# A 32-expert clamped-SwiGLU layer: the gate's activation reads PSUM before the clamp, and one product moves ahead of a subtraction

## Chip, cores and metric

The kernel is one launch on 1 core of one Trainium2 chip. The metric is device time in microseconds; lower is better. The engines are named as in the profile: PE (TensorE matmuls) and PEld (its weight loads), DVE (VectorE), ACT (ScalarE), POOL (GpSimd) and SP (SyncE).

## The reference

One decoder layer for 520 tokens (512 of a prompt, 8 sampled): a recurrent branch and an attention branch, merged by an output projection, then a mixture of 32 experts of which each token takes 4. The change lies in the experts and in one step before them. What an expert computes:

```python
gu = t_pad[tok] @ w_up[e] + b_up[e]
a = jnp.minimum(gu[:, :D_FF], 7.0)
u = jnp.clip(gu[:, D_FF:], -7.0, 7.0)
y = ((u + 1.0) * a * jax.nn.sigmoid(1.702 * a)) @ w_down[e] + b_down[e]
```

`D_MODEL` and `D_FF` are 1024, so an expert has 2048 columns of `w_up` (gate and up part) and 1024 of `w_down`: 12 MB of float32, six slots of 2 MB each.

## The kernel before, in words

**Before the experts.** After the attention and the recurrent branch PE multiplies by the output projection, tile of rows by tile of rows (`RT` is 5; tile 0 holds the 8 sampled tokens). DVE adds the residual (`residual`, L2171), ACT squares and takes the root (L1535, L1543), PE turns the rows (L1021) and computes the router's logits (L1032), DVE picks the four experts of each token. In tile 0 the up bias, fetched into `oT` by two DMAs of POOL's queue (L2438, semaphore `bup_in`), is split into a rounded high part (ACT, L1576 and L1577) and a remainder (DVE, L2274); PE adds both to a chunk with one matmul (L1142).

**The experts.** Each expert takes the rows of its tokens (at most 128) and multiplies in float32 by splitting every operand in a rounded high part and a low part (three products for each). The weights come as six slots of 2 MB (`c` = 0 to 5, each in two halves `h`), read by 192 DMAs from SP's queue. For each of the 12 halves ACT rounds the half into a work tile (`high_half`, L1555; the tile names are `xn`, `wide` and `qT` by turns) and DVE subtracts it in place (`low_half`, L2253). Chunks 0 to 3 are the up projection: chunk 0 makes the first 512 gate columns in PSUM bank 0, chunk 1 the matching up columns in bank 1, chunks 2 and 3 the second 512 of each in banks 2 and 3 (PE, L1150, 24 matmuls a chunk). Chunks 4 and 5 are the down projection (L1168, 12 matmuls a half).

The hidden values are made in two halves `hf`:

- `gate_part(n, hf)` (DVE, L2296): minimum with 7 of the gate bank into `AA`.
- `gated(n, hf)` (ACT, L1595): `Gelu_apprx_sigmoid` of `AA` into `SG`, that is a·sigmoid(1.702a).
- `hidden_part(n, hf)` (DVE): the up bank is clamped to ±7 into `UU[hf]` (L2300), then (UU + 1)·SG in place (L2303).
- PE turns `UU[hf]` (`turn_hidden`, L1132), ACT rounds it (`turned_hidden`, L1599), DVE subtracts (`low_hidden`, L2307).

Nothing schedules this: every engine runs an order written out by hand, with semaphores between them. PE's order for expert `n` (`block_of`) is: chunks 0, 1, 2; turn 0; chunk 3; half (4,0); turn 1; half (4,1); then it waits until both parts of the second hidden half are there (`hh_ready` and `hl_ready` at 2n+2), turns the next expert's rows (`turn_rows`, L1126, 8 transposes) and does (5,0) and (5,1). The wait is written ahead of `turn_rows`:

```python
down_half(n, 4, 1)
pe.wait_ge(S["hh_ready"], 2 * n + 2)
pe.wait_ge(S["hl_ready"], 2 * n + 2)
if following:
    turn_rows(n + 1, 1 - par)
down_half(n, 5, 0)
```

DVE's `hidden_part(n, 1)` waits until PE is through with chunk 3 (`half_used` at 12n + 20). `following` is true for the experts 0 to 30. A branch for an expert with over 128 tokens follows the experts; with these inputs it is not taken.

Of the kernel before, what the change touches and what calls it, by code (L numbers as in the profile page):

```python
# [9 lines left out]
ALU = mybir.AluOpType  # L10
ACT = mybir.ActivationFunctionType
# [8 lines left out]
D = 1024  # L20
# [37 lines left out]
EPS = 1e-6  # L58
LIMIT = 7.0
ALPHA = 1.702  # L60
SLOT = 4096
NSLOT = 6
ROUTER_IN = 96
# [26 lines left out]
def build(nc, d):  # L90
    ctx = ExitStack()
    with ctx:
# [87 lines left out]
        def w8(name):  # L180
# [123 lines left out]
        XH, XL, HH, HL = [slab_r[:, (2 + b) * D:(3 + b) * D].rearrange("p (k t) -> p k t", k=KD) for b in range(4)]  # L304
        XHf, HHf = [slab_r[:, (2 + b) * D:(3 + b) * D].bitcast(F32) for b in (0, 2)]
        YR = [slab[:, (6 + b) * D:(7 + b) * D] for b in (0, 1)]
        AA = slab[:, 8192:8704]
        SG = slab[:, 8704:9216]
        UU = [slab[:, 9216 + b * 512:9728 + b * 512] for b in (0, 1)]
        pick_r = slab_r[:, 10304:10432]  # L310
        pick = causal[:, 0:NE]
# [25 lines left out]
            gate_done gate_out pa_done pb_done m_ready  # L337
            wo_done router_in xm_ready row_norm t_ready x_picked oh_ready t_turned t_copied lg_done ex_in ex_done gd_ready gd_turned
            gd_copied bd_done y0_ready m4_ready pos_done ent_ready table_in scattered bup_in ovf_ready
            bias_hi bias_ready pick_set  # L340
            xg_in ent_in gate_set rows_free x_turned xh_ready xl_ready half_used up_read sig_ready h_ready h_turned hh_ready hl_ready
            wh_ready wl_ready y_scaled y_added
            outs_done""".split()}
# [218 lines left out]
        def _(pe):  # L562
# [570 lines left out]
                r.then_inc(S["h_turned"], 1)  # L1133

            def up_chunk(n, c, last_biases=False):
                pe.wait_ge(S["up_read"], 4 * n + c + 1)
                if c == 0:
                    pe.wait_ge(S["pick_set"], n + 1)
                    pe.wait_ge(S["xh_ready"], n + 1)
                    pe.wait_ge(S["xl_ready"], n + 1)  # L1140
                q = order[c]
                mm(bank[:, c, :], pick_r, bias_r[:, q * 512:(q + 1) * 512], start=True, stop=False)  # L1142
                for h in range(2):
                    pe.wait_ge(S["wh_ready"], 12 * n + 2 * c + h + 1)
                    pe.wait_ge(S["wl_ready"], 12 * n + 2 * c + h + 1)
                    wh = WH[(2 * c + h) % 6].rearrange("p (k n) -> p k n", k=4)
                    wl = ring_r[:, half_of(c, h)].rearrange("p (k n) -> p k n", k=4)
                    for k in range(4):
                        for x, (a, w) in enumerate(((XH, wh), (XH, wl), (XL, wh))):
                            r = mm(bank[:, c, :], a[:, 4 * h + k, :], w[:, k, :], start=False,  # L1150
                                   stop=h == 1 and k == 3 and x == 2)
                    r.then_inc(S["half_used"], 1)
                    if last_biases and h == 0:
                        down_bias(RT - 2, 1)
                        down_bias(RT - 1, 0)
                        down_bias(RT - 1, 1)
# [52 lines left out]
        def _(act):  # L1209
# [347 lines left out]
            for t in range(RT):  # L1557
                if t >= 1:
                    turned_part(t - 1, 1)
                row_squares(t, 0)  # L1560
                if t >= 1:
                    chosen(t - 1)
                if t == RT - 1:
                    fn(lt[:, 0, 0:1], eps1[:, 0:1], ACT.Sqrt)
                turned_part(t, 0)
                if t == RT - 1:
                    turned_gates(t - 1)
                row_squares(t, 1)
                if t == RT - 1:
                    turned_part(t, 1)  # L1570
                row_root(t)
                if 1 <= t < RT - 1:
                    turned_gates(t - 1)
                if t == 0:
                    act.wait_ge(S["bup_in"], 32)
                    fn(bias_r[0:NE, :], bias_raw[0:NE, :], ACT.Copy).then_inc(S["bias_ready"], 1)  # L1576
                    fn(WH[0][NE:2 * NE, :], bias_raw[NE:2 * NE, :], ACT.Copy).then_inc(S["bias_hi"], 1)  # L1577
                if t == 2:
                    act.wait_ge(S["bias_ready"], 3)
                if t in (2, 3):  # L1580
                    high_half(0, 0, t - 2)
# [9 lines left out]
                fn(XH, bank[:, 6:8, :].rearrange("p b (k t) -> p (b k) t", k=4), ACT.Copy).then_inc(S["xh_ready"], 1)  # L1591

            def gated(n, hf):
                act.wait_ge(S["up_read"], 4 * n + 2 * hf + 5)
                fn(SG, AA, ACT.Gelu_apprx_sigmoid).then_inc(S["sig_ready"], 1)  # L1595

            def turned_hidden(n, hf):
                act.wait_ge(S["h_turned"], 2 * n + hf + 1)
# [37 lines left out]
            high_half(0, 1, 1)  # L1636
            high_half(0, 2, 0)
            act.wait_ge(S["bd_done"], 2 * RT)
            block_of(0, 0, True)
            block_of(1, 1, True)  # L1640
            with act.Fori(1, NE // 2 - 1) as pair:
# [15 lines left out]
        def _(dve):  # L1657
# [3 lines left out]
            def one(ins, sem=None):  # L1661

                mine(ins, sem)
                mine.settle()
# [590 lines left out]

            one(v.tensor_tensor(pick, ident[:, 0:NE], ident[:, NE:2 * NE], ALU.add))
            one(v.memset(first_oh[1], 0.0))
            for t in range(RT):
                residual(t, 0)
                if t >= 2:  # L2260
# [9 lines left out]
                row_scale(t)  # L2270
                normalise(t)
                if t == 0:
                    dve.wait_ge(S["bias_hi"], 1)
                    v.tensor_tensor(bias_r[NE:2 * NE, :], bias_raw[NE:2 * NE, :], WHf[0][NE:2 * NE, :], ALU.subtract)\  # L2274
                        .then_inc(S["bias_ready"], 1)
                if t in (2, 3):
# [1 line left out]
            choose(RT - 1)  # L2278
            positions(RT - 1)
            to_weigh(RT - 1)  # L2280
            dve.sem_inc(S["up_read"], 2)

            def low_rows(n):
                dve.wait_ge(S["xh_ready"], n + 1)
# [6 lines left out]
            def pick_expert(e):  # L2291
                v.tensor_copy(pick_r, pick[:, bass.ds(e, 1)].to_broadcast([P, P])).then_inc(S["pick_set"], 1)

            def gate_part(n, hf):
                dve.wait_ge(S["half_used"], 12 * n + 4 * hf + 14)
                v.tensor_scalar(AA, bank[:, 2 * hf, :], LIMIT, None, ALU.min).then_inc(S["up_read"], 1)  # L2296

            def hidden_part(n, hf):
                dve.wait_ge(S["half_used"], 12 * n + 4 * hf + 16)
                v.tensor_scalar(UU[hf], bank[:, 2 * hf + 1, :], LIMIT, -LIMIT, ALU.min, ALU.max).then_inc(S["up_read"], 1)  # L2300
                dve.wait_ge(S["up_read"], 4 * n + 2 * hf + 6)
                dve.wait_ge(S["sig_ready"], 2 * n + hf + 1)
                v.scalar_tensor_tensor(UU[hf], UU[hf], 1.0, SG, ALU.add, ALU.mult).then_inc(S["h_ready"], 1)  # L2303

            def low_hidden(n, hf):
                dve.wait_ge(S["hh_ready"], 2 * n + hf + 1)
# [10 lines left out]
            def block_of(n, e, following, par=None):  # L2317
                low_half(n, 2, 0)
                low_half(n, 2, 1)
                dve.wait_ge(t_out[0], 48)  # L2320
                dve.wait_ge(t_out[1], 32)
                dve.wait_ge(y0_out[2], 16)
                gate_part(n, 0)
                low_half(n, 3, 0)
                low_half(n, 3, 1)
                hidden_part(n, 0)
                low_half(n, 4, 0)
                low_half(n, 4, 1)
                gate_part(n, 1)
                dve.wait_ge(y0_out[0], 32)  # L2330
                low_hidden(n, 0)
                low_half(n, 5, 0)
                low_half(n, 5, 1)
                hidden_part(n, 1)
                if following:
                    pick_expert(e + 1)
                    low_half(n + 1, 0, 0)
# [14 lines left out]
            dve.wait_ge(S["pos_done"], RT + 1)  # L2352
            one(v.tensor_reduce(ovf[:, 0:1], bank[:, 2, 0:NE], AX, ALU.max))
            one(v.tensor_copy(ovf[:, 1:2].bitcast(I32), ovf[:, 0:1]), S["ovf_ready"])
            dve.sem_inc(S["up_read"], 1)
            first_rows(RT - 2, 0)
            low_half(0, 1, 0)
            first_rows(RT - 2, 1)
            dve.sem_inc(S["up_read"], 1)
            low_half(0, 1, 1)  # L2360
            first_rows(RT - 1, 0)
            first_rows(RT - 1, 1)
            with dve.Fori(0, NE // 2 - 1) as pair:
                block_of(2 * pair, 2 * pair, True, 0)
                block_of(2 * pair + 1, 2 * pair + 1, True, 1)
# [306 lines left out]
```

## Time and profile before

| | us |
|---|---|
| median of 3 runs | 1887.18 |
| lowest, highest | 1885.93, 1888.0 |
| span of the profiled execution (first to last instruction) | 1886.3 |
| PE busy | 1827.4 (97%) |
| DVE busy | 1502.2 (80%) |
| ACT busy | 1130.4 (60%) |

For the profiled execution the page gives the span as its time; the median of the runs is 0.9 us above it. The experts take the last 1175 us of the span, from PE's first bias matmul at 712.3 us on. Busy time is a mean over stages with different limits; in a row of a timeline the columns are start, duration, engine, line, operation, what is written and read, and in brackets the idle time of the engine before it with what ended it. The matmuls of a sequence overlap: one of 512 columns lasts 0.39 us in the rows, and the next starts 0.23 us after it.

### The profile page before, as it was taken

How to read it: one execution, taken by the hardware profiler on the slowest of the kernel's cores; microseconds unless marked ns; L12 is line 12 of the kernel's file. 1: busy time of each engine (PE TensorE's matmuls, PEld its weight loads, DVE VectorE, ACT ScalarE, POOL GpSimd, SP SyncE). 2: the span in 40 equal slices, each digit the busy share in tenths (PEclk: the TensorE clock that was granted, in tenths of full speed). 3: DMA queues.
4: the chain of work that ended last, by engine and by line, in shares of the span. 5: the costliest groups of instructions: out<-in, count | busy, mean ns of one | idle time of the engine just before them, and what ended most of it. 6: DMA issues, size and time to landing. Idle time of an engine off the chain costs nothing.

```text
span 1886.3 us, 27452 instructions
## 1 busy us (share of the span) xinstructions
PE 1827.4 (97%) x9813; PEld 1500.9 (80%) x9813; DVE 1502.2 (80%) x1754; ACT 1130.4 (60%) x1126; POOL 239.8 (13%) x259
## 2 busy tenths in 40 slices
PE   7999999999999999999999999999999999999996
PEld 5899988787767677888888888888888888888885
DVE  6865875654367468999999999999999999999994
ACT  5335555442332346767767767776777776776772
POOL 0040000012331131100100110010010010010000
PEclk9999999999999999999999999999999999999998
DMA  5075221132355258999999999999999999999991
GB/s 226 8 247 164 70 78 46 49 94 82 113 167 197 72 199 347 358 396 382 372 381 389 372 375 385 374 377 385 380 372 380 387 370 380 387 374 381 382 365 43
DMA packets 76748, 514.23 MB, mean 273 GB/s; under 512 B 10745, under 2 KB 31297, under 8 KB 50801
## 3 DMA queue, kind: packets, MB, share of 16 engines
q1 hardware_dynamic: 58944, 454.19, 61.4%
q0 software_dynamic: 17584, 58.51, 11.5%
q8 instruction: 46, 0.75, 0.2%
q10 hardware_dynamic: 144, 0.55, 0.1%
q14 instruction: 30, 0.24, 0.0%
HBM read 490.36 MB, written 28.24 MB: 275 GB/s over the span
## 4 chain that ended last, share of the span: by engine, by line
PE 75%; issue 8%; DVE 7%; ACT 6%; DMA 3%; SPq 0%; ACTq 0%; DVEq 0%; POOL 0%; POOLq 0%
PE bank L1150 27%; PE bank L1168 14%; PE bank L700 6%; PE bank L752 5%; PE bank L627 3%; ACT qT_rounded L1555 3%; PE bank L600 3%; PE bank L999 3%; PE bank L1132 2%; PE bank L1126 1%; PE bank L974 1%; DVE slab L2300 1%; DVE slab L2303 1%; PE bank L1142 1%; PE bank L765 1%
## 5 line engine op out<-in xcount | busy, mean ns | idle before, releaser
L2253 DVE TENSOR_TENSOR ring_rounded<-ring,wide_rounded 128x2048 fp32r<-128x2048 f32 x192 | 431.4, 2288 | 50.8 <-ACT wide_rounded L1555 50.3
L1150 PE MATMUL bank<-ring_rounded,slab_rounded 128*128 128x512 f32 x1024 | 400.2, 391 | 0.0
L1555 ACT ACTIVATE wide_rounded<-ring 128x2048 fp32r<-128x2048 f32 x192 | 359.8, 1908 | 10.3 <-PE bank L1150 8.7
L1150 PE MATMUL bank<-xn_rounded,slab_rounded 128*128 128x512 f32 x1024 | 326.3, 389 | 0.0
L2253 DVE TENSOR_TENSOR ring_rounded<-ring,xn_rounded 128x2048 fp32r<-128x2048 f32 x128 | 293.0, 2289 | 17.1 <-ACT xn_rounded L1555 17.1
L1168 PE MATMUL bank<-wide_rounded,slab_rounded 128*128 128x512 f32 x768 | 259.7, 399 | 0.0
L1150 PE MATMUL bank<-wide_rounded,slab_rounded 128*128 128x512 f32 x768 | 247.3, 389 | 0.0
L1555 ACT ACTIVATE xn_rounded<-ring 128x2048 fp32r<-128x2048 f32 x128 | 244.0, 1906 | 0.0
L1150 PEld LDWEIGHTS bank<-ring_rounded,slab_rounded 128*128 128x128 f32 x1024 | 192.2, 188 | 41.3
L1150 PEld LDWEIGHTS bank<-xn_rounded,slab_rounded 128*128 128x128 f32 x1024 | 192.3, 188 | 40.1 <-issue 0.8
L2480 POOL DMA_INDIRECT out_y<-slab,small x32 | 85.0, 2656 | 999.9 <-ACT slab L1630 999.9
L1168 PE MATMUL bank<-ring_rounded,slab_rounded 128*128 128x512 f32 x512 | 200.6, 392 | 0.0
L1599 ACT ACTIVATE slab_rounded<-bank 128x512 fp32r<-128x512 f32 x64 | 38.3, 599 | 221.5 <-PE bank L1132 221.5
L1150 PEld LDWEIGHTS bank<-wide_rounded,slab_rounded 128*128 128x128 f32 x768 | 144.2, 188 | 31.2
L1168 PEld LDWEIGHTS bank<-wide_rounded,slab_rounded 128*128 128x128 f32 x768 | 145.0, 189 | 29.0
L700 PE MATMUL bank<-ring_rounded 128*128 128x260 f32 x768 | 148.1, 292 | 2.3 <-DVE slab_rounded L1873 2.3
L2253 DVE TENSOR_TENSOR ring_rounded<-ring,qT_rounded 128x2048 fp32r<-128x2048 f32 x64 | 146.5, 2290 | 0.9
L700 PEld LDWEIGHTS bank<-ring_rounded 128*128 128x128 f32 x768 | 117.9, 188 | 16.7 <-issue 11.9
L1555 ACT ACTIVATE qT_rounded<-ring 128x2048 fp32r<-128x2048 f32 x64 | 122.3, 1912 | 1.9 <-PE bank L1082 1.9
L1168 PEld LDWEIGHTS bank<-ring_rounded,slab_rounded 128*128 128x128 f32 x512 | 96.7, 189 | 18.7
L600 PE MATMUL bank<-ring_rounded 128*128 128x260 f32 x512 | 95.0, 287 | 2.8 <-ACT small L1332 2.0
L1168 PE MATMUL bank<-qT_rounded,slab_rounded 128*128 128x512 f32 x256 | 85.4, 394 | 0.0
(463 smaller groups left out, 2983.5 us busy)
## 6 DMA issues: line engine op xcount, KB each, us to landing
ring<-in_w_exp SPq DMA_DIRECT2D x192, 2048.0 KB, 10.5
ring<-in_w_blk SPq DMA_DIRECT2D x40, 512.0 KB, 3.6
slab<-in_w_tok SPq DMA_DIRECT2D x4, 1304.0 KB, 15.3
ring<-in_w SPq DMA_DIRECT2D x8, 512.0 KB, 3.7
ring<-in_w_out SPq DMA_DIRECT2D x2, 2048.0 KB, 14.3
xn<-in_xT SPq DMA_DIRECT2D x4, 520.0 KB, 8.2
ring<-in_k_cmp SPq DMA_DIRECT2D x32, 64.0 KB, 3.5
ring<-in_k_cmp POOLq DMA_DIRECT2D x32, 64.0 KB, 2.8
```

The source lines that it names most:

```text
L600: r = mm(bank[:, banks + h, 0:HN], w[:, k, wcols], a[:, k, cols], start=first and x == 0, stop=last and x == 2)
L627: r = mm(out, u[:, k, q], w[:, k, a:b], start=k == 0 and x == 0, stop=k == KD - 1 and x == 2)
L700: r = mm(bank[:, 6 + h, 0:HN], w[:, k, :], a[:, k, cols], start=k == 0 and y == 0, stop=k == KD - 1 and y == 2)
L752: r = mm(bank[:, 4 * h + 2 * f + x, :].rearrange("p (g c) -> p g c", g=NPAGES), w[:, f, x, :], a, start=l == 0 and y == 0, stop=l == LP - ...
L999: return mm(out, three[0][x][k][:, a:a + n], w[:, k, :], start=first, stop=last)
L1132: r = pe.transpose(bank[:, 6 + hf, f * P:(f + 1) * P], UU[hf][:, f * P:(f + 1) * P], ident[:, :])
L1150: r = mm(bank[:, c, :], a[:, 4 * h + k, :], w[:, k, :], start=False, stop=h == 1 and k == 3 and x == 2)
L1168: r = mm(bank[:, 4 + y, :], a[:, k, :], w[:, f, cols], start=k == 0 and x == 0, stop=k == KD - 1 and x == 2)
L1555: fn(WH[(2 * c + h) % 6], ring[:, half_of(c, h)], ACT.Copy).then_inc(S["wh_ready"], 1)
L1599: fn(HH[:, 4 * hf:4 * hf + 4, :], bank[:, 6 + hf, :].rearrange("p (f t) -> p f t", f=4), ACT.Copy)\
L2253: v.tensor_tensor(ring_r[:, half_of(c, h)], ring[:, half_of(c, h)], WHf[(2 * c + h) % 6], ALU.subtract)\
L2480: pool.indirect_dma_start(out=d["y"][:, :], out_offset=bass.IndirectOffsetOnAxis(ap=index, axis=0), in_=YR[par], in_offset=None, compute_o ...
```

## The change

1. `gate_part` is gone. ACT reads the gate's PSUM bank itself, as soon as PE is through with the gate chunk, into `SG[hf]` (two buffers now: the old `AA` and `SG`).
2. The clamp of the gate is put behind the activation: since x·sigmoid(1.702x) rises above its minimum, the minimum with its value at 7 (`GATE_LIMIT`) is the same. It is folded into DVE's product.
3. The 1 of (u + 1) is added to the up part's bias beforehand, by a new DVE instruction on `oT` before the loop over tiles; the clamp is then to -6 and 8. DVE now waits for `bup_in` there.
4. In DVE's `block_of`, `hidden_part(n, 1)` stands ahead of `low_half(n, 5, 1)`; before, it stood behind it.
5. PE's waits for free banks go by `sig_ready` (gate banks) and `up_read` (up banks). Waits for the DMAs that free the shared memory (`t_out`, `y0_out`) move from within DVE's `block_of` to before the loop, and ACT gets two of them.

```diff
+GATE_LIMIT = LIMIT / (1.0 + math.exp(-ALPHA * LIMIT))
-        AA = slab[:, 8192:8704]
-        SG = slab[:, 8704:9216]
+        SG = [slab[:, 8192 + b * 512:8704 + b * 512] for b in (0, 1)]
             def up_chunk(n, c, last_biases=False):
-                pe.wait_ge(S["up_read"], 4 * n + c + 1)
+                if isinstance(n, int) and n == 0:
+                    if c >= 2:
+                        pe.wait_ge(*((S["ovf_ready"], 1), (S["y0_ready"], 2 * RT - 2))[c - 2])
+                else:
+                    pe.wait_ge(S["up_read" if c % 2 else "sig_ready"], 2 * n + c // 2 - 1)
...
             def gated(n, hf):
-                act.wait_ge(S["up_read"], 4 * n + 2 * hf + 5)
-                fn(SG, AA, ACT.Gelu_apprx_sigmoid).then_inc(S["sig_ready"], 1)
+                act.wait_ge(S["half_used"], 12 * n + 4 * hf + 14)
+                fn(SG[hf], bank[:, 2 * hf, :], ACT.Gelu_apprx_sigmoid).then_inc(S["sig_ready"], 1)
...
             act.wait_ge(S["bd_done"], 2 * RT)
+            act.wait_ge(t_out[0], 48)
+            act.wait_ge(y0_out[2], 16)
...
             one(v.memset(first_oh[1], 0.0))
+            dve.wait_ge(S["bup_in"], 32)
+            v.tensor_scalar(bias_raw[0:2 * NE, D:2 * D], bias_raw[0:2 * NE, D:2 * D], 1.0, None, ALU.add).then_inc(S["bias_step"], 1)
             for t in range(RT):
                 residual(t, 0)
...
-            def gate_part(n, hf):
-                dve.wait_ge(S["half_used"], 12 * n + 4 * hf + 14)
-                v.tensor_scalar(AA, bank[:, 2 * hf, :], LIMIT, None, ALU.min).then_inc(S["up_read"], 1)
-
             def hidden_part(n, hf):
                 dve.wait_ge(S["half_used"], 12 * n + 4 * hf + 16)
-                v.tensor_scalar(UU[hf], bank[:, 2 * hf + 1, :], LIMIT, -LIMIT, ALU.min, ALU.max).then_inc(S["up_read"], 1)
-                dve.wait_ge(S["up_read"], 4 * n + 2 * hf + 6)
+                v.tensor_scalar(UU[hf], bank[:, 2 * hf + 1, :], 1.0 + LIMIT, 1.0 - LIMIT, ALU.min, ALU.max).then_inc(S["up_read"], 1)
+                dve.wait_ge(S["up_read"], 2 * n + hf + 1)
                 dve.wait_ge(S["sig_ready"], 2 * n + hf + 1)
-                v.scalar_tensor_tensor(UU[hf], UU[hf], 1.0, SG, ALU.add, ALU.mult).then_inc(S["h_ready"], 1)
+                v.scalar_tensor_tensor(UU[hf], SG[hf], GATE_LIMIT, UU[hf], ALU.min, ALU.mult).then_inc(S["h_ready"], 1)
...
             def block_of(n, e, following, par=None):
                 low_half(n, 2, 0)
                 low_half(n, 2, 1)
-                dve.wait_ge(t_out[0], 48)
-                dve.wait_ge(t_out[1], 32)
-                dve.wait_ge(y0_out[2], 16)
-                gate_part(n, 0)
                 low_half(n, 3, 0)
                 low_half(n, 3, 1)
                 hidden_part(n, 0)
                 low_half(n, 4, 0)
                 low_half(n, 4, 1)
-                gate_part(n, 1)
                 dve.wait_ge(y0_out[0], 32)
                 low_hidden(n, 0)
                 low_half(n, 5, 0)
+                hidden_part(n, 1)
                 low_half(n, 5, 1)
-                hidden_part(n, 1)
                 if following:
                     pick_expert(e + 1)
                     low_half(n + 1, 0, 0)
```

The lines of the changed kernel are numbered a little higher: L2253 becomes L2259, L2300 and L2303 become L2303 and L2306, L2307 becomes L2310, L2171 becomes L2177.

DVE, expert 30, from the subtraction of half (5,0) to the next expert's first subtraction and the hidden one behind it. Before:

```order
L2253 TENSOR_TENSOR ring_rounded<-ring,wide_rounded 128x2048
L2253 TENSOR_TENSOR ring_rounded<-ring,qT_rounded 128x2048
L2300 TENSOR_SCALAR slab<-bank 128x512
L2303 SCALAR_TENSOR_TENSOR slab<-slab 128x512
L2292 CAST slab_rounded<-small 128x128
L2253 TENSOR_TENSOR ring_rounded<-ring,xn_rounded 128x2048
L2289 COPY small<-small 128x1
L2307 TENSOR_TENSOR slab_rounded<-bank,slab_rounded 128x512
```

The changed kernel, the same stretch:

```order
L2259 TENSOR_TENSOR ring_rounded<-ring,wide_rounded 128x2048
L2303 TENSOR_SCALAR slab<-bank 128x512
L2306 SCALAR_TENSOR_TENSOR slab<-slab 128x512
L2259 TENSOR_TENSOR ring_rounded<-ring,qT_rounded 128x2048
L2299 CAST slab_rounded<-small 128x128
L2259 TENSOR_TENSOR ring_rounded<-ring,xn_rounded 128x2048
L2296 COPY small<-small 128x1
L2310 TENSOR_TENSOR slab_rounded<-bank,slab_rounded 128x512
```

Between the clamp of the up bank and the hidden subtraction there was one subtraction of 2048 columns, (31,0,0), and now there are two, (30,5,1) and (31,0,0).

DVE, the end of the branch merge and the first residual of the output projection, in the changed kernel:

```order
L2164 CAST oT_rounded<-ident 64x2048
L2166 TENSOR_TENSOR qT<-qT 128x256
L2262 TENSOR_TENSOR small<-ident 128x32
L2263 MEMSET kT 128x128
L2265 TENSOR_SCALAR oT<-oT 64x1024
L2177 SCALAR_TENSOR_TENSOR slab<-bank,wide 8x512 x2
```

The instruction at L2265 is new; all others stand as before, and both residual additions of tile 0 come behind it.

## Rows read from the trace of the kernel before

**Rows 1.** The page, busy time of each engine over the span

```profile
PE 1827.4 (97%) x9813; PEld 1500.9 (80%) x9813; DVE 1502.2 (80%) x1754; ACT 1130.4 (60%) x1126; POOL 239.8 (13%) x259
```

**Rows 2.** Timeline of PE: start, duration, then as above; turn 0 of expert 14

```profile
1239.89 0.60 PE L1132 MATMUL bank<-ident,slab 128*128 128x128 f32 x4
1240.24 0.48 PE L1142 MATMUL bank<-oT_rounded,slab_rounded 128*128 128x512 f32 x1
```

**Rows 3.** Timeline of PE, same expert, end of chunk 3 to the next expert's rows

```profile
1245.78 0.39 PE L1150 MATMUL bank<-xn_rounded,slab_rounded 128*128 128x512 f32 x1
...
1248.50 0.39 PE L1168 MATMUL bank<-wide_rounded,slab_rounded 128*128 128x512 f32 x1
1249.04 0.66 PE L1132 MATMUL bank<-ident,slab 128*128 128x128 f32 x4 [0.16 <-DVE slab L2303]
1249.46 0.47 PE L1168 MATMUL bank<-wide_rounded,slab_rounded 128*128 128x512 f32 x1
...
1252.29 1.07 PE L1126 MATMUL bank<-ident,slab 128*128 128x128 f32 x8
```

**Rows 4.** Timeline of DVE, same stretch

```profile
1242.96 2.29 DVE L2253 TENSOR_TENSOR ring_rounded<-ring,wide_rounded 128x2048 fp32r<-128x2048 f32 x1 [1.04 <-ACT wide_rounded L1555]
1245.28 2.29 DVE L2253 TENSOR_TENSOR ring_rounded<-ring,qT_rounded 128x2048 fp32r<-128x2048 f32 x1
1247.49 0.69 DVE L2300 TENSOR_SCALAR slab<-bank 128x512 f32<-128x512 f32 x1
1248.30 0.69 DVE L2303 SCALAR_TENSOR_TENSOR slab<-slab 128x512 f32<-128x512 f32 x1
1248.90 0.22 DVE L2292 CAST slab_rounded<-small 128x128 fp32r x1
1249.04 2.29 DVE L2253 TENSOR_TENSOR ring_rounded<-ring,xn_rounded 128x2048 fp32r<-128x2048 f32 x1
...
1251.31 0.68 DVE L2307 TENSOR_TENSOR slab_rounded<-bank,slab_rounded 128x512 fp32r<-128x512 f32 x1
```

**Rows 5.** The line L1126 on PEld: count, duration, first and last start

```profile
L1126 PEld LDWEIGHTS bank<-ident,slab x248: 138/141/143, 748.7 to 1828.3; 128*128 128x128 f32 x124
```

**Rows 6.** Timelines of PE and DVE, expert 0, around its turn 1

```profile
741.37 0.39 PE L1168 MATMUL bank<-wide_rounded,slab_rounded 128*128 128x512 f32 x1
744.11 1.12 PE L1132 MATMUL bank<-ident,slab 128*128 128x128 f32 x4 [2.35 <-DVE slab L2303]
744.88 0.78 PE L1168 MATMUL bank<-wide_rounded,slab_rounded 128*128 128x512 f32 x1
...
742.54 0.69 DVE L2300 TENSOR_SCALAR slab<-bank 128x512 f32<-128x512 f32 x1
```

**Rows 7.** Stretches: length, busy time, then granted clock, DMA share, GB/s

```profile
184.70:570.00 385.30, 370.66 (x2643) 306.05 (x2644) 232.15 (x561) 165.81 (x337) 53.24 (x100) 1.00 0.30 88
...
744.80:748.20 3.40, 3.40 (x11) 2.76 (x11) 2.76 (x4) 2.40 (x2) 0.00 (x0) 0.60 0.78 324
```

**Rows 8.** Timeline of PE, the longest idle time in the first of these stretches

```profile
420.50 0.50 PE L752 MATMUL bank<-xn_rounded,hidden_high 128*128 128x512 f32 x1 [2.31 <-DVE ring_rounded L1883]
```

**Rows 9.** The up bias: its DMAs on POOL's queue, and their time to landing

```profile
612.18 1.01 POOL L2438 DMA_DIRECT2D oT<-in_b_up x2 [23.38 <-DVE slab L2150]
...
DMA to landing us min/median/max: 6.4/6.6/6.7
```

**Rows 10.** Timelines of DVE, PE and ACT in tile 0 of the output projection

```profile
613.33 1.22 DVE L2158 CAST oT_rounded<-ident 64x2048 fp32r<-64x2048 f32 x1
...
620.33 0.68 DVE L2171 SCALAR_TENSOR_TENSOR slab<-bank,wide 8x512 f32<-8x512 f32 x1 [4.13 <-PE bank L999]
...
620.16 0.41 PE L1021 MATMUL bank<-ident,slab 8*128 8x8 f32 x4
627.49 0.63 PE L1032 MATMUL bank<-qT,wide 128*8 128x32 f32 x16 [0.59 <-ACT wide L1529]
...
621.05 0.63 ACT L1535 ACTIVATE kT<-slab 8x512 f32<-8x512 f32 x1 [0.24 <-DVE slab L2171]
```

More of the change, by code:

```diff
@@ L339, in build @@
             gd_copied bd_done y0_ready m4_ready pos_done ent_ready table_in scattered bup_in ovf_ready
-            bias_hi bias_ready pick_set
+            bias_step bias_ready pick_set
             xg_in ent_in gate_set rows_free x_turned xh_ready xl_ready half_used up_read sig_ready h_ready h_turned hh_ready hl_ready
@@ L1574, in _ @@
                 if t == 0:
-                    act.wait_ge(S["bup_in"], 32)
+                    act.wait_ge(S["bias_step"], 1)
                     fn(bias_r[0:NE, :], bias_raw[0:NE, :], ACT.Copy).then_inc(S["bias_ready"], 1)
-                    fn(WH[0][NE:2 * NE, :], bias_raw[NE:2 * NE, :], ACT.Copy).then_inc(S["bias_hi"], 1)
+                    fn(WH[0][NE:2 * NE, :], bias_raw[NE:2 * NE, :], ACT.Copy).then_inc(S["bias_step"], 1)
                 if t == 2:
@@ L2272, in _ @@
                 if t == 0:
-                    dve.wait_ge(S["bias_hi"], 1)
+                    dve.wait_ge(S["bias_step"], 2)
                     v.tensor_tensor(bias_r[NE:2 * NE, :], bias_raw[NE:2 * NE, :], WHf[0][NE:2 * NE, :], ALU.subtract)\
@@ L2280, in _ @@
             to_weigh(RT - 1)
-            dve.sem_inc(S["up_read"], 2)
             def low_rows(n):
@@ L2354, in _ @@
             one(v.tensor_copy(ovf[:, 1:2].bitcast(I32), ovf[:, 0:1]), S["ovf_ready"])
-            dve.sem_inc(S["up_read"], 1)
             first_rows(RT - 2, 0)
@@ L2358, in _ @@
             first_rows(RT - 2, 1)
-            dve.sem_inc(S["up_read"], 1)
             low_half(0, 1, 1)
@@ L2362, in _ @@
             first_rows(RT - 1, 1)
+            dve.wait_ge(t_out[0], 48)
+            dve.wait_ge(t_out[1], 32)
+            dve.wait_ge(y0_out[2], 16)
             with dve.Fori(0, NE // 2 - 1) as pair:
```

## The prediction

> **What bounds the kernel now.** The page's busy shares come first [rows 1]: PE 97%, DVE 80%, ACT 60%. A DVE with a fifth of its time free might seem not to matter, but shares are means, so next I read one expert of the steady part on PE and DVE side by side. The starts of the rows' transposes give the period: 248 of them, 8 an expert, so 31 experts, the first group at 748.7 us and the last at 1828.3 us [rows 5]; (1828.3 - 748.7) / 30 = 35.99 us an expert. PE issues nearly without a pause in it. In [rows 3] the reader is to see where it does pause: the last matmul of half (4,0) starts at 1248.50, so the next slot would be 0.23 later, at 1248.73, and turn 1 starts only at 1249.04. It waited for DVE's product, which ended at 1248.30 + 0.69 = 1248.99 [rows 4]. So DVE holds PE up once an expert, by 0.31 us, and a start on PE follows the end on DVE by 0.05 us.
>
> The second thing to see is what is nearly late. PE waits for the hidden subtraction (L2307) before `turn_rows`. That subtraction ends at 1251.31 + 0.68 = 1251.99 [rows 4], and PE's transposes start at 1252.29 with no pause ahead (the matmul before them started at 1252.06). Their weight load runs ahead of the matmul by up to 0.2 us, so the slack is under 0.1 us of 36. Whatever delays L2307 on DVE relative to PE delays the whole expert.
>
> **The change, part by part.**
>
> *Two minima go.* Each took about 0.69 us on DVE, the next instruction following at 0.60, so 1.2 us an expert. In front of the clamp of the second up bank this frees nothing: that clamp must wait for PE's chunk 3. The subtraction of (5,0) starts at 1242.96 because ACT's rounding ended then, not because of DVE's queue the 1.04 us idle of [rows 4], and it ends at 1245.25. Chunk 3's last matmul starts at 1245.78 and ends at 1246.17 [rows 3]. So now DVE will sit idle for about 1 us and start the clamp at 1246.17 + 0.05 = 1246.22 (it was 1247.49). Worth 0, hidden by PE's chunk 3; likewise ACT reading the bank: the activation can start about a us sooner, but DVE needs it no sooner.
>
> *The product moves ahead of the subtraction of (5,1).* The product starts 0.81 after the clamp, at 1247.03, and ends at 1247.72. PE asks for it at 1248.73: the wait of 0.31 us goes, and with it 0.07, as the four transposes and the switch take 0.42 us after the wait (1249.04 to 1249.46, [rows 3]) but 0.35 without one (1239.89 to 1240.24, [rows 2]). PE would reach `turn_rows` at 1252.29 - 0.38 = 1251.91.
>
> *What is late next.* Between the clamp and L2307 stand now two subtractions of 2048 columns instead of one, since (5,1) is behind the product and the next expert's (0,0) stays where it was. From the clamp's start, in steps of [rows 4]: 0.81 to the product, 0.60 to what follows it, 2.21 for subtraction (5,1) (1245.28 to 1247.49), 0.14 for the expert's pick (1248.90 to 1249.04), 2.27 for (0,0) and the gate column (1249.04 to 1251.31), and 0.68 for L2307 itself: 6.71 us. So L2307 ends at 1246.22 + 6.71 = 1252.93, and PE's transposes start at 1252.98 instead of 1252.29. PE has a new wait of 1252.98 - 1251.91 = 1.07 us in place of the old of 0.38, **0.69 us more an expert**. Queued behind it on PE are `turn_rows` and (5,0); ACT's rounding of the next rows and everything after are released by PE, so they shift along and nothing gives the time back. DVE and ACT have slack in the rest of the period, the more for the minima that went.
>
> Where the 0.69 holds: experts 1 to 30, that is 30 times: +20.7 us. Bounds: the register instruction between clamp and product goes, so the product could follow at 0.69 instead of 0.81 (-0.12 an expert, 17.1 us in all); and the transposes may pay the 0.07 after a wait (22.8 us). I take 20.7, the rows as they are.
>
> *Expert 0.* Here DVE comes late from the router: PE could have begun turn 1 at 741.37 + 0.23 = 741.60 and began at 744.11, and for a while afterwards its clock was granted at 0.60 on the mean, that is partly at the lower level of 1.2 GHz [rows 6, 7]. DVE's clamp began at 742.54 [rows 6]; without one subtraction (2.21) and the two minima (1.2) ahead of it, it begins at 739.1, just when chunk 3 ends (12 matmuls of 0.23 before 741.60). Then this expert behaves as the others: turn 1 at 741.60, `turn_rows` 3.18 later but for the wait (1252.29 - 1249.04 - 0.07), plus 1.07: 745.85 instead of 748.7 to 748.95. Worth -3.0 us; bounds -3.3, and -1.4 if the clock falls there all the same.
>
> *Expert 31* has no next expert, so no (0,0) ahead of its L2307: 2.35 us less, no new wait. It keeps the gain: -0.3 us (0.2 to 0.4).
>
> *The 1 in the bias.* DVE waits for both bias DMAs before the first residual. They are issued at 612.18, the second about 0.5 later, and take 6.6 us [rows 9]: landed at about 619.3. The trace has no add of this shape. One source of 64x2048 in SBUF took 1.22 us [rows 10], so 1024 columns 0.61 at least; the clamp took 0.69 for 512 columns from PSUM [rows 4], so 1.3 at most. I take 0.65, by the row whose source is in SBUF too. The Trainium skill (VectorE: DVE Perf Modes, on why a single-source operation gets two results a cycle for fp32) puts an add of a constant with both ends in SBUF at the faster rate and one from PSUM at the slower; by that rule it is the lower end, and the cast's row agrees with it.
>
> So the first residual ends at about 620.7 instead of before 620.16, when PE used it [rows 10], and the second at 621.4 instead of 621.01. PE is late by 0.5 at L1021, and ACT, whose two squarings used to lie apart, does them back to back from 620.7 on, so the second starts about 0.9 late (it was 621.05). PE waits for ACT at L1032 already (0.59 idle, [rows 10]), so that lateness lands on the path: +1.0 us, bounds 0.4 and 1.8. All other waits put before the loops (`t_out`, `y0_out`) are for transfers issued some 10 us and more earlier: 0.
>
> **Sum.** 20.7 - 3.0 - 0.3 + 1.0 = +18.4 us on the profiled 1886.3 us: 1904.7. The runs' median stands 0.9 above that profile, so **1905.6 us**, 1.0% slower. The bounds together give 17.1 - 3.3 - 0.4 + 0.4 = +13.8 and 22.8 - 1.4 - 0.2 + 1.8 = +23.0, or 1901 to 1910. A measurement of this kernel can tell about 0.2% (3.8 us) from no change.
>
> **Rivals.**
>
> 1. *Faster: the removed wait is all there is.* Place: L2307 of experts 0 to 30. It decides at 1251.91 - 1246.22 - 0.05, about 5.6 us from the clamp to L2307's end: if DVE needs less, PE finds it done. Then -0.38 x 30 = -11.4, expert 0 reaches `turn_rows` at 744.8 (-4.0), -0.3 and +1.0: -14.7, or 1872.5. For it: slack was there before, and DVE is 80% busy. Against it: 6.71 us are five instructions whose durations hardly vary, and the clamp cannot start before chunk 3 ends. 7 in 100.
> 2. *About even.* The stretch comes out near 6.1 us, with half the new wait: +0.1 an expert, in all 1885 to 1895. It needs the instructions to overlap better than in [rows 4]. 6 in 100.
> 3. *The clock falls at the new waits.* The stretch of 3.40 us at a granted clock of 0.60 [rows 7] lost 1.4 us, and the transposes at its head 0.35 (0.77 from 744.11 to 744.88 against 0.42). Thirty times 1.7 more is +51: 1956. Against it: that fall came with 2.5 us idle, and a pause of 2.31 us at 420.50 [rows 8] lies in a stretch with clock 1.00 [rows 7]. The new pause is 1.07. The Trainium skill (TensorE: Matmul & The Clock Gate, on avoiding throughput drops) warns that idle gaps between bursts of matmuls bring the clock back to half; [rows 6, 7] agree that they can, [rows 8] that a pause twice the new one need not. 4 in 100.
> 4. *A longer wait than I see*, say if the subtraction of (5,1) slows beside ACT: 1912 to 1920. 3 in 100.
>
> **The numbers.** The forecast gets 80 in 100. Its own range 1901 to 1910 is stretched by 2 us at either end for the rows' rounding over thirty repetitions: 1899 to 1912; outside lie the rivals, 2 in 10. Faster by over 0.2%: rival 1 and a little of 2, 0.08. Within 0.2%: most of 2 below 1891, 0.04. Slower: 0.88.
>
> **What would show it.** Right: transposes of L1126 at a period of 36.6 to 36.75; idle time of PE before them put down to DVE's hidden subtraction, about 30 times with 0.7 to 1.1 each; none before L1132; DVE idle about 1 us before the clamp, released by PE; and no fall of the granted clock after 725 us. Wrong: a period of 35.6 (rival 1), or L2307 ending less than 6 us after the clamp's start. The start would be wrong if PE's first row transposes of tile 0 stood at 620.2 as before.

## The result, and the profile after

| | before | changed |
|---|---|---|
| median of 4 runs, us | 1886.56 | 1907.43 |
| lowest, highest | 1885.82, 1888.0 | 1906.3, 1907.79 |
| span of the profiled execution | 1886.3 | 1905.6 (its own time 1907.22) |

The ratio of the runs is 1.0107, 95% interval 1.0095 to 1.0119: the change makes the kernel 1.1% slower. Forecast were 1905.6 us and 1899 to 1912. The kernel before has four runs here; the median of 1887.18 that the forecast starts from was that of the first three.

The busy line of the page, against [rows 1]: DVE has 63 instructions and 39.5 us of work less, and still the kernel is longer.

```profile
PE 1824.0 (96%) x9813; PEld 1500.9 (79%) x9813; DVE 1462.7 (77%) x1691; ACT 1131.3 (59%) x1126; POOL 243.2 (13%) x259
```

The timeline of PE, the stretch of [rows 3] in the changed kernel (half (4,0) ends, turn 1, half (4,1) ends, row transposes):

```profile
1251.30 0.39 PE L1154 MATMUL bank<-xn_rounded,slab_rounded 128*128 128x512 f32 x1
...
1254.02 0.39 PE L1172 MATMUL bank<-wide_rounded,slab_rounded 128*128 128x512 f32 x1
1254.24 0.60 PE L1132 MATMUL bank<-ident,slab 128*128 128x128 f32 x4
...
1257.21 0.39 PE L1172 MATMUL bank<-wide_rounded,slab_rounded 128*128 128x512 f32 x1
1258.59 1.09 PE L1126 MATMUL bank<-ident,slab 128*128 128x128 f32 x8 [0.99 <-DVE slab_rounded L2310]
```

Turn 1 follows the last matmul at once: the old wait is gone. The pause stands before the row transposes now: the next slot after 1257.21 would be 1257.44, the transposes start at 1258.59, so 1.15 us are lost there. The timeline of DVE in the same stretch, against [rows 4]:

```profile
1251.72 0.69 DVE L2303 TENSOR_SCALAR slab<-bank 128x512 f32<-128x512 f32 x1 [0.95 <-PE bank L1154]
1252.45 0.69 DVE L2306 SCALAR_TENSOR_TENSOR slab<-slab 128x512 f32<-128x512 f32 x1
1253.06 2.29 DVE L2259 TENSOR_TENSOR ring_rounded<-ring,qT_rounded 128x2048 fp32r<-128x2048 f32 x1
1255.26 0.22 DVE L2299 CAST slab_rounded<-small 128x128 fp32r x1
1255.39 2.29 DVE L2259 TENSOR_TENSOR ring_rounded<-ring,xn_rounded 128x2048 fp32r<-128x2048 f32 x1
1257.60 0.15 DVE L2296 COPY small<-small 128x1 f32 x1
1257.66 0.68 DVE L2310 TENSOR_TENSOR slab_rounded<-bank,slab_rounded 128x512 fp32r<-128x512 f32 x1
```

The clamp waits 0.95 us for PE's chunk 3, which ends at 1251.30 + 0.39 = 1251.69; two subtractions of 2.2 us follow the product, and the hidden subtraction ends at 1258.34. PE starts 0.25 us after that. The row transposes (L1126) on PE over all experts, and what ended the idle time before them:

```profile
L1126 PE MATMUL bank<-ident,slab x248: 272/273/326, 743.8 to 1847.8; 128*128 128x128 f32 x124
its engine sat idle before it (us, times) until:
  DVE slab_rounded L2310: 27.7, 28
  issue: 2.5, 3
```

So PE pauses there 31 times. 28 of the pauses, 0.99 us idle each, are put down to L2310; the three that the view calls "issue" (0.84 us each) are those in experts 0, 1 and 30, which stand outside the loop over experts. The last time of such a line is the start of the last single instruction, the eighth of its group and 0.8 us after the group's start. So 30 periods are 1847.8 - 743.8 - 0.8 = 1103.2 us, 36.77 each. Before, by the same rule, they were 35.96 (the 35.99 of the prediction missed the 0.8 us).

Where the 19.3 us of the spans lie, by the starts of PE's groups:

| stretch | before | changed | difference |
|---|---|---|---|
| start to the experts' first bias matmul | 712.3 | 708.9 | -3.4 |
| expert 0, to its row transposes | 36.6 | 34.9 | -1.8 |
| experts 1 to 30 | 1078.7 | 1103.2 | +24.5, 0.82 each |
| from there to the end | 58.6 | 58.6 | 0.0 |

The first line is for the most part no effect of the change. By 610 us, up to where both kernels run the same instructions, the changed one is 1.5 us ahead already. Between 610 and 634 us it loses 0.9 us, at the new bias add. Behind that it gains 2.8 us: the granted clock was at its lower level from 640.2 to 643.6 and from 701.7 to 705.1 us there, and in the kernel before from 638.3 to 645.1 and from 703.1 to 710.0 us, twice as long. In the experiments below that start lies anywhere between 708.9 and 717.2 us, and mostly it is the later the longer PE ran at the lower level beforehand (13.7 to 30.7 us in all). Rows of the stretch from 500 us to the first bias matmul (last three columns: granted clock, DMA share, GB/s), of the changed kernel, of the kernel before and of `e1_product_back`:

```profile
500.00:708.90 208.90, 199.17 (x1236) 150.70 (x1235) 125.24 (x308) 72.57 (x119) 48.19 (x71) 0.98 0.44 151
```

```profile
500.00:712.30 212.30, 203.37 (x1242) 154.63 (x1241) 125.17 (x309) 73.74 (x121) 49.14 (x72) 0.96 0.44 151
```

```profile
500.00:714.80 214.80, 205.10 (x1242) 155.14 (x1241) 125.81 (x310) 73.50 (x121) 49.10 (x72) 0.95 0.44 150
```

So single executions are best compared by their expert stretch, and whole times by their medians.

### The profile page after: what moved, and what is told of

The parts are those of the page before. It is cut to its first block, busy times and chain, and to the rows that moved or that the text cites. A ratio compares the mean times of both kernels' runs of the same rounds, so it can differ in the third digit from the quotient of the medians.

```text
span 1905.6 us, 27158 instructions
## 1 busy us (share of the span) xinstructions
PE 1824.0 (96%) x9813; PEld 1500.9 (79%) x9813; DVE 1462.7 (77%) x1691; ACT 1131.3 (59%) x1126; POOL 243.2 (13%) x259
## 4 chain that ended last, share of the span: by engine, by line
PE 79%; DVE 11%; issue 5%; DMA 2%; ACT 2%; DVEq 0%; SPq 0%; POOL 0%; ACTq 0%; POOLq 0%
PE bank L1154 37%; PE bank L1172 10%; PE bank L700 6%; PE bank L752 5%; DVE ring_rounded L2259 3%; PE bank L627 3%; PE bank L600 3%; PE bank L999 2%; PE bank L1126 2%; PE bank L1146 2%; PE bank L765 1%; PE bank L786 1%; DVE slab L2303 1%; DMA slab<-in_w_tok 1%; DVE slab_rounded L2310 1%
## 5 line engine op out<-in xcount | busy, mean ns | idle before, releaser
L2259 DVE TENSOR_TENSOR ring_rounded<-ring,wide_rounded 128x2048 fp32r<-128x2048 f32 x192 | 431.3, 2287 | 51.1 <-ACT wide_rounded L1559 50.4
L2259 DVE TENSOR_TENSOR ring_rounded<-ring,xn_rounded 128x2048 fp32r<-128x2048 f32 x128 | 289.8, 2284 | 1.6 <-ACT xn_rounded L1559 1.6
L2259 DVE TENSOR_TENSOR ring_rounded<-ring,qT_rounded 128x2048 fp32r<-128x2048 f32 x64 | 146.2, 2285 | 0.0
L2303 DVE TENSOR_SCALAR slab<-bank 128x512 f32<-128x512 f32 x64 | 44.3, 692 | 53.7 <-PE bank L1154 53.7
```

What stands on the lines that cost most here:

```text
L2259: v.tensor_tensor(ring_r[:, half_of(c, h)], ring[:, half_of(c, h)], WHf[(2 * c + h) % 6], ALU.subtract)\
L2303: v.tensor_scalar(UU[hf], bank[:, 2 * hf + 1, :], 1.0 + LIMIT, 1.0 - LIMIT, ALU.min, ALU.max).then_inc(S["up_read"], 1)
```

## The experiments

The theory: the loss is the second subtraction that now stands between the clamp and the hidden subtraction. The rivals: the loss comes with the fused activation (ACT reading the bank, the folded clamp, the changed waits), or the distance from DVE's end to PE's start is of another kind. Periods are the mean of the 30 intervals between the row transposes. Each ratio is to the kernel before as it ran in the same round (medians 1887.49, 1887.61 and 1887.5 us).

| kernel | median us | ratio to before, 95% interval | period |
|---|---|---|---|
| changed | 1907.43 | 1.0107 (1.0095 to 1.0119) | 36.77 |
| e1_product_back | 1880.38 | 0.9962 (0.9948 to 0.9976) | 35.84 |
| e2_before_product_ahead | 1913.72 | 1.0132 (1.0117 to 1.0148) | 36.87 |
| e3_hidden_ahead | 1876.27 | 0.9931 (0.9915 to 0.9946) | 35.59 |
| e4_rows_wait_first | 1904.7 | 1.0097 (1.008 to 1.0115) | 36.67 |
| e5_two_subtractions | 2017.27 | 1.0685 (1.0669 to 1.07) | 40.32 |
| e6_before_both | 1874.41 | 0.9925 (0.991 to 0.994) | 35.59 |
| e7_before_hidden_ahead | 1888.17 | 0.9999 (0.999 to 1.0008) | 35.96 |
| e8_both_bias_late | 1872.86 | 0.9925 (0.9913 to 0.9936) | 35.59 |
| e9 (e6 again) | 1871.39 | 0.9923 (0.991 to 0.9937) | 35.59 |
| e10 (e8 again) | 1872.9 | 0.992 (0.9906 to 0.9934) | 35.59 |

**Undo the move alone (e1_product_back).** In the changed kernel:

```diff
                 low_half(n, 5, 0)
-                hidden_part(n, 1)
                 low_half(n, 5, 1)
+                hidden_part(n, 1)
```

> The change with only the second product put back behind the subtraction of (5,1). Theory 1 (the loss is the second subtraction between the clamp and the hidden subtraction L2310): the new pause of PE before the row transposes goes, the old wait before turn 1 comes back at about 0.23 us (the clamp-to-product spacing is 0.72 now instead of 0.81), the period is 35.88 us as against 36.79 in the change and 35.96 before; expert 0 gains 1.3 us from the minima that went. Time 1883 to 1886, against about 1886.6 of before and 1907.4 of the change. Theory 2 (the loss comes from ACT reading PSUM, or from the folded clamp and the changed waits): the time stays near 1907.

Measured 1880.38 us (1879.01 to 1883.5). The loss is gone, and the rest of the change is a gain of 0.4%. The period is 35.84 us:

```profile
L1126 PE MATMUL bank<-ident,slab x248: 270/273/277, 747.9 to 1823.8; 128*128 128x128 f32 x124
```

Of the 0.12 us against before, 0.09 are the product that follows its clamp sooner; for the rest the clamp itself starts 0.03 us sooner after the end of chunk 3 (1.29 us against 1.32). In the timeline of DVE of this kernel:

```profile
1209.11 0.68 DVE L2303 TENSOR_SCALAR slab<-bank 128x512 f32<-128x512 f32 x1
1209.83 0.69 DVE L2306 SCALAR_TENSOR_TENSOR slab<-slab 128x512 f32<-128x512 f32 x1
```

They are 0.72 apart, and 0.81 in [rows 4]. There the waits for `up_read` and `sig_ready` have different values, and the trace has a register instruction for the second (L2302, 1248.21 to 1248.25 us) behind the first wait, between the end of the clamp and the product. In the changed kernel both values are the same, and that instruction is done while the clamp runs. No run changes this alone, so the reason for the 0.09 us is read from the trace and not shown by an experiment. The time is below what was expected (1883 to 1886): expert 0 took 33.2 us here against 36.6 before. PE idled 0.65 us before its turn 1 instead of 2.35, and the granted clock did not fall there (before, it was at the lower level from 744.1 to 747.5 us, which costs half of these 3.4 us). The expectation had counted the wait and not the clock.

**The move alone (e2_before_product_ahead).** The kernel before, with the diff above turned round.

> The kernel before with only the second product put ahead of the subtraction of (5,1); both minima and the activation stay as they were. Theory 1: the whole loss is here: clamp to L2307's end 6.71 us, PE starts 0.25 us after it, period 36.85 to 36.9 us; expert 0 gains 1.2 us less than in the change. Time 1908 to 1912. Theory 2 (the loss needs the fused activation): stays at 1886.

Measured 1913.72 us (1910.91 to 1914.04), period 36.87. The whole loss is in the move of one line: without the fused activation it is even larger, as the 0.81 spacing stays. PE's pause before the row transposes:

```profile
1227.21 1.09 PE L1126 MATMUL bank<-ident,slab 128*128 128x128 f32 x8 [1.08 <-DVE slab_rounded L2307]
```

Theory 2 falls with these two runs.

**One subtraction less behind the product (e3_hidden_ahead).** In the changed kernel:

```diff
                 if following:
                     pick_expert(e + 1)
-                    low_half(n + 1, 0, 0)
                 if par is not None:
                     dve.wait_ge(S["ent_in"], 16)
                     gate_column(e, par)
                 low_hidden(n, 1)
                 if following:
+                    low_half(n + 1, 0, 0)
                     low_half(n + 1, 0, 1)
```

> The change, with the hidden subtraction (L2310) and the gate column ahead of the next expert's subtraction (0,0) instead of behind it. Theory 1: clamp to L2310's end is 4.4 us, less than the 5.7 that PE needs from chunk 3's end to the row transposes, so neither wait is left: period 35.58 us, expert 0 four us better than before. Time 1871 to 1874. Theory 2 (subtraction (0,0), now later, is the next to be waited for, or ACT's rounding of the hidden half comes too late): a new wait of PE at chunk 0 or at the transposes, period 35.8 or more, time 1880 or more.

Measured 1876.27 us (1871.55 to 1879.09). The period is 35.59, the 35.58 expected, and neither wait is left. The list of waits of this kernel between 900 and 1800 us has no entry of PE or of its weight loads:

```profile
POOL out_y L2479 <- ACT slab L1634: 806.5, 26, 31.2
ACT slab_rounded L1603 <- PE bank L1132: 165.4, 50, 4.3
DVE slab L2303 <- PE bank L1154: 36.2, 50, 1.0
ACT wide_rounded L1559 <- PE bank L1154: 34.8, 51, 0.8
ACT slab_rounded L1595 <- PE bank L1126: 30.6, 25, 1.2
DVE slab_rounded L2310 <- ACT slab_rounded L1603: 26.7, 25, 1.1
DVE ring_rounded L2259 <- ACT wide_rounded L1559: 26.2, 25, 1.0
POOL slab L2470 <- issue: 7.6, 25, 0.3
ACT slab L1599 <- PE bank L1154: 4.9, 26, 0.2
```

Its median lies 2 us above the expected 1871 to 1874. In the profiled execution the experts began late, at 717.2 us, and the clock fell once in expert 0; its period leaves no other place for it.

**PE's own share of the pause (e4_rows_wait_first).** In the changed kernel (and no wait in `turn_rows` there):

```diff
                 down_half(n, 4, 1)
+                if following:
+                    pe.wait_ge(S["xg_in"], 16 * (n + 1))
                 pe.wait_ge(S["hh_ready"], 2 * n + 2)
                 pe.wait_ge(S["hl_ready"], 2 * n + 2)
                 if following:
-                    turn_rows(n + 1, 1 - par)
+                    turn_rows(n + 1, 1 - par, False)
```

> The change, with PE's wait for the gathered rows (xg_in) ahead of its waits for hh_ready and hl_ready instead of behind them. In the trace of the change PE starts its transposes 0.24 us after L2310's end inside the loop, where a register instruction of PE's queue lies between the waits, and 0.10 us after it where the loop is unrolled. Theory A (the register instruction behind the last wait is what costs the difference): 0.10 to 0.15 everywhere, period 36.64 to 36.7 us, time 1903 to 1905. Theory B (the distance has another cause): period 36.79, time 1907.4.

Measured 1904.7 us (1903.73 to 1912.52), period 36.67: theory A. The hidden subtraction and PE's transposes, first in the timeline of DVE, then of PE:

```profile
1220.18 0.68 DVE L2313 TENSOR_TENSOR slab_rounded<-bank,slab_rounded 128x512 fp32r<-128x512 f32 x1
```

```profile
1221.00 1.06 PE L1127 MATMUL bank<-ident,slab 128*128 128x128 f32 x8 [0.89 <-DVE slab_rounded L2313]
```

1221.00 - 1220.86 = 0.14 us, against 1258.59 - 1258.34 = 0.25 in the changed kernel. The median moved by 2.7 us, which its range (up to 1912.5) does not settle; the single periods do. All 30 are 36.66 to 36.68 us here. In the changed kernel 27 are 36.78 or 36.79, and only the three that begin or end in an expert outside the loop, where the wait has a constant for its value, are shorter (36.61, 36.75 and 36.64).

**Twice the cost (e5_two_subtractions).** The changed kernel with `low_half(n + 1, 0, 1)` ahead of `low_hidden(n, 1)` too:

```diff
                     low_half(n + 1, 0, 0)
+                    low_half(n + 1, 0, 1)
                 if par is not None:
...
                 low_hidden(n, 1)
                 if following:
-                    low_half(n + 1, 0, 1)
                     low_rows(n + 1)
```

> The change, with one subtraction more (the next expert's (0,1)) ahead of the hidden subtraction L2310: the suspected cost doubled. Theory 1: the pause of PE before the row transposes grows by one subtraction, 2.2 us, to about 3.4 us, period 39.0 us, time 1971 to 1976. The rival on the clock: pauses of 3.4 us bring the granted clock to its lower level in most experts; then about 1.7 us more for each, up to 2024, and a mean clock well below 0.99.

Measured 2017.27 us (2016.19 to 2025.43). Both the added subtraction and the fall of the clock show, one on top of the other. Of the 30 periods 5 are 38.98 to 39.00 us, the 39.0 of theory 1; the other 25 are 40.3 to 40.7, 1.6 us more, and there the clock fell. Two experts with the same pause, in the timeline of PE, and the granted clock after each (stretch rows of both):

```profile
877.15 1.09 PE L1126 MATMUL bank<-ident,slab 128*128 128x128 f32 x8 [3.20 <-DVE slab_rounded L2310]
...
917.73 1.09 PE L1126 MATMUL bank<-ident,slab 128*128 128x128 f32 x8 [3.19 <-DVE slab_rounded L2310]
```

```profile
877.40:882.00 4.60, 4.60 (x19) 3.73 (x18) 2.10 (x2) 3.73 (x3) 0.00 (x0) 0.63 0.78 331
...
917.40:922.00 4.60, 4.27 (x23) 3.68 (x24) 1.59 (x3) 3.15 (x3) 0.00 (x0) 1.00 0.86 349
```

After the first the mean granted clock is 0.63, partly the lower level of 1.2 GHz, and 19 matmuls fall in 4.6 us; after the second it is 1.00 and 23 do, though 0.33 us of the pause lie in that stretch. The five periods without a fall do not lie at random: they are the 5th, 11th, 16th, 21st and 26th. No run shows what sets this beat. The arithmetic closes: against the changed kernel 30 x 2.21 = 66.3 for the subtraction and 25 x 1.6 = 40 for the clock make 106.3, and the 30 experts are 1209.6 - 1103.2 = 106.4 us longer.

In the changed kernel the pause is a third of that and costs no clock:

```profile
725.00:1800.00 1075.00, 1046.58 (x4797) 857.30 (x4796) 938.86 (x615) 765.83 (x527) 117.43 (x59) 1.00 0.97 371
```

**Both moves without the fusion (e6_before_both), and one of them (e7_before_hidden_ahead).** The kernel before, with the product ahead of (5,1) and the hidden subtraction ahead of (0,0); and with the second of these alone.

> The kernel before, with the second product ahead of (5,1) and the hidden subtraction ahead of (0,0), but with the minima and the activation as they were. If the order alone makes the gain of the version with both: period 35.58 us as there, expert 0 some 1.2 to 2 us later, no late start of the merge: time 1872 to 1875. If the fused activation is needed for it (DVE short of time with the two minima): a period of 35.8 or more, time 1880 or more.

> The kernel before, with only the hidden subtraction ahead of the next expert's (0,0). The wait before turn 1 stays (0.31 us), the hidden subtraction was just in time already: period 35.9 to 36.0, time 1885 to 1888, no difference. Rival: the slack of under 0.1 us at L2307 was in truth a wait, then up to 0.2 us an expert is gained: 1880 to 1883.

e6: 1874.41 us, period 35.59. e7: 1888.17, ratio 0.9999, period 35.96. So the order alone makes the gain, each move is worth nothing or a loss by itself, and together they are worth 0.36 us an expert. DVE's 1.2 us an expert from the fused activation are worth nothing once PE sets the period.

**The bias add later (e8_both_bias_late).** e3 with the add behind both residuals of tile 0:

```diff
-            dve.wait_ge(S["bup_in"], 32)
-            v.tensor_scalar(bias_raw[0:2 * NE, D:2 * D], bias_raw[0:2 * NE, D:2 * D], 1.0, None, ALU.add).then_inc(S["bias_step"], 1)
             for t in range(RT):
...
                 residual(t, 1)
                 if t >= 2:
                     first_rows(t - 2, 1)
+                if t == 0:
+                    dve.wait_ge(S["bup_in"], 32)
+                    v.tensor_scalar(bias_raw[0:2 * NE, D:2 * D], bias_raw[0:2 * NE, D:2 * D], 1.0, None, ALU.add).then_inc(S["bias_step"], 1)
                 row_scale(t)
```

> The change with the hidden subtraction ahead of (0,0), and the add of 1 to the bias behind both residual additions of tile 0 instead of ahead of them. PE's pause of 0.79 us before the first row transposes of tile 0 (L1021) goes, and ACT squares as early as before: 0.5 to 1.0 us less than the version with only the hidden subtraction ahead, which is near what a run's time scatters by (2 us). In the profile the idle time before L1021 is what decides.

Measured 1872.86 us (1870.2 to 1875.26). The times overlap with e3's; the profile decides. The first row transposes of tile 0 on PE, in the changed kernel and in e8:

```profile
619.49 0.38 PE L1021 MATMUL bank<-ident,slab 8*128 8x8 f32 x4 [0.79 <-DVE slab L2177]
```

```profile
617.82 0.41 PE L1021 MATMUL bank<-ident,slab 8*128 8x8 f32 x4
```

The pause of 0.79 us is gone.

**Does the fusion pay at all (e9_before_both_again, e10_both_bias_late_again)?** e6 and e8 again, side by side.

> The kernel before with both instructions moved (product ahead of (5,1), hidden subtraction ahead of (0,0)), timed again beside the next run. The order alone makes the gain: period 35.59 us, time within 1871 to 1878.

> The change with the hidden subtraction ahead and the late bias add, timed again beside the kernel before with both moves. Theory 1 (PE sets the period of both, so the fused activation is worth nothing in experts 1 to 31 and about 0.6 us in expert 0): a difference of 0 to 1 us, not told apart from none by their ranges. Rival (the 1.2 us an expert that DVE gains is worth something): at least 0.1 us an expert, 3 us or more below the other, with a shorter period.

1871.39 us (1870.4 to 1875.35) without the fusion and 1872.9 (1871.25 to 1874.56) with it: no difference that can be told, and the same period of 35.59. In expert 0 the fusion can be seen: without a fall of the clock in it, it took 32.8 us in e9 and 32.3 in e8, near the 0.6 us expected. Both kernels beat the kernel before by 0.8%. The simplest kernel of the best time is the kernel before with two lines moved.

## Why the prediction was right

- **The clamp waits for chunk 3.** Right: 0.95 us idle released by PE, and a start 0.03 us after its end (0.05 assumed). The minima that went gave nothing in the steady part, as said; e9 and e10 confirm it.
- **The old wait goes.** Right, 0.38 us: none before turn 1 in any expert.
- **The new wait.** Right in place and kind: two subtractions, then L2310, then PE. Predicted +0.69 us an expert, measured +0.82 (36.77 against 35.96). Three terms were off. The start of PE after DVE's end was taken as 0.05, from turn 1, and is 0.25 here: +0.20. The clamp-to-product spacing fell from 0.81 to 0.73, which the prediction had only in its lower bound: -0.08. The transposes take 0.84 us to the next matmul after a wait and 0.80 without, which it had only in its upper bound: +0.04. Two more differences (the clamp's start and the rest of the chain) take 0.03 back, which closes the 0.13. Of the 0.20, 0.11 are shown by e4 to be the order of PE's own waits: behind the one for the hidden subtraction stood another, whose value a register instruction first works out. With that wait in front the distance is 0.14; what the other 0.09 against turn 1 are stays open. The start is the mis-sized term, worth 6 us over 30 experts, and the prediction held the sign of it: it called the slack of L2307 under 0.1 us where PE started 0.30 us after its end, which leaves over 0.2 us for the start, and then took 0.05 in the sum.
- **Expert 0.** Predicted -3.0, measured -1.8. DVE was in time, as worked out (its clamp waited for PE), and the wait of 2.5 us went, but the clock fell once in this expert in the changed kernel's profile as well, only in chunk 0 (715.3 to 718.7 us). PE had no idle time just before that fall; six matmuls of L1082 (32x512, 2.8 us together) stood there, as they do in e8, where it did not fall. In e8, where it did not fall there, expert 0 took 32.3 us, against 33.8 with a fall in e3: 1.5 us. The prediction's bound of -1.4 allowed for that.
- **Expert 31.** Predicted -0.3: from its predecessor's row transposes to its last scaling on ACT it took 41.40 us instead of 41.66. From there to the end it took 0.23 us more, so that nothing is left of it in the table. From the last row transposes to the end the twelve profiled executions take 58.3 to 58.8 us, and no run shows why.
- **The bias.** Predicted +1.0; the pause shows 0.79, and between 610 and 634 us the changed kernel loses 0.9 us on the kernel before. ACT's later squarings cost nothing more: PE's wait before L1032 was 0.59 and became 0.63. The add took 0.69 us for 0.65.
- **The other waits put before the loops.** Said to be free because their transfers were issued long before. The cost is nothing in the end, but the reason was wrong: one was not done, and ACT waited 5.2 us for it in expert 0. In the timeline of ACT of the changed kernel:

```profile
718.04 1.92 ACT L1559 ACTIVATE qT_rounded<-ring 128x2048 fp32r<-128x2048 f32 x1 [5.19 <-DMA out_y<-slab]
```

  It was issued at 700.76 and landed 17 us later; from 709 to 715 us the DMA engines' share was 1.00. PE did not feel it: its next pause is that before the row transposes at 743.80.
- **The number.** That it came so near is in part luck. In the experts the forecast was +17.4 us (20.7 - 3.0 - 0.3) and the measured difference +22.7 (24.5 - 1.8 + 0.0), 5.3 us more. Ahead of them the forecast was +1.0 and the measured difference -3.4, mostly from the clock, which no term held. So the span grew by 19.3 us, against 18.4 forecast; the medians show +20.9. With the 5.3 us alone the forecast would have been 1910.9 us, still in the stated range. Whether the changed kernel starts its experts early as a rule is open: its four runs lie within 1.5 us, but e4, the same up to there, had one run of five at 1912.5 us.
- **Rivals.** Rival 1 (only the removed wait) and rival 2 fell with the period. Rival 3 (the clock) did not come about at a pause of 1.15 us; e5 shows that it does at 3.4 us, at the price named, 1.6 for the 1.7 assumed. But one reason given against it was weaker than it looked. The pause of 2.31 us of [rows 8] was followed by no fall in the kernel before; in 7 of the 12 profiled executions the clock fell right after this same pause, whose instructions no edit touches. In `e7_before_hidden_ahead`, first the timeline of PE, then the stretch row behind it with a clock of 0.50:

```profile
420.57 0.72 PE L752 MATMUL bank<-xn_rounded,hidden_high 128*128 128x512 f32 x1 [2.31 <-DVE ring_rounded L1883]
```

```profile
420.80:424.00 3.20, 3.20 (x8) 2.53 (x8) 3.20 (x4) 1.29 (x2) 3.20 (x7) 0.50 0.97 272
```

  So one execution without a fall did not show that a pause twice the new one is free. What does speak against rival 3 are the pauses of 1.1 us themselves: 31 each in the profiles of the changed kernel and of e4, none followed by a fall.
- **The lines on the Trainium skill.** Its warning about idle gaps between bursts of matmuls (TensorE: Matmul & The Clock Gate, on avoiding throughput drops) agrees with 25 of the 30 pauses of e5 and not with the other 5. For the bias its rule on single-source operations (VectorE: DVE Perf Modes, on why a single-source operation gets two results a cycle for fp32) agrees with 0.69 us for 1024 columns in SBUF, the time the clamp takes for 512 from PSUM.

## What to carry to other kernels

When an instruction is moved ahead on an engine that is not the bottleneck, count what now stands between the event that releases it and every later result that the bottleneck waits for: here, counted from the end of chunk 3, the product was done 1.4 us earlier and the hidden subtraction 0.8 us later. The first saved PE 0.38 us an expert, the second cost it 1.2. Move the whole chain that the bottleneck waits for, or nothing: two moved lines gained 0.8%, and 1.2 us less work an expert on DVE gained 0.4% in the old order (e1) and nothing that can be told on top of the two moves. If an engine waits on several semaphores, put the one that comes last at the end, with no other wait behind it whose value has to be worked out.

## What was not expected of the hardware

- A wait whose value comes from a register instruction behind another wait costs 0.11 us at each pass (0.25 against 0.14 us from DVE's end to PE's start, changed kernel and e4). On DVE two dependent instructions stand 0.81 us apart with such an instruction between them and 0.72 to 0.73 without; no run isolates that.
- The same pause of 3.2 us was followed by a fall of the granted clock in 25 of 30 experts and not in the other 5, at regular distances (e5), at 1.6 us a fall; one of 2.3 us was in 7 of 12 executions. So what such a pause costs can be told on the mean of many, not for one.
- The twelve profiled executions reach the experts' first bias matmul at 708.9 to 717.2 us, mostly by their falls of the clock before that; the bias add, the one difference of their code up to there, is worth 0.9 us. An effect of under 2 us is found in a stage's timeline and hardly in the medians of five runs.
